# Layer 0's experts: VectorE's 32x32 block transposes in place of TensorE's products by the identity

## The reference

```python
def expert_choice_ffn(h, router_w, router_b, w_gate, w_up, w_down):
    cap = EC_CAPACITY * n // N_EXPERTS            # 64 latent rows, 32 context rows an expert
    affinity = jax.nn.softmax((h @ router_w + router_b).astype(F32), axis=-1)
    gates, idx = lax.top_k(jnp.swapaxes(affinity, 1, 2), cap)
    xg = jax.vmap(lambda hb, ib: hb[ib])(h, idx)
    hid = jax.nn.silu(jnp.einsum('becd,edf->becf', xg, w_gate)) * jnp.einsum('becd,edf->becf', xg, w_up)
    y = jnp.einsum('becf,efd->becd', hid, w_down) * gates[..., None].astype(h.dtype)
    scatter = lambda yb, ib: jnp.zeros((n, d), h.dtype).at[ib.reshape(-1)].add(yb.reshape(-1, d))
    return jax.vmap(scatter)(y, idx)
...
        f_l = expert_choice_ffn(modulate(rmsnorm(x, ...), mod_l[3], mod_l[4]), ...)
        if ctx_out:                               # layer 0 only
            f_c = expert_choice_ffn(modulate(rmsnorm(ctx, ...), mod_c[3], mod_c[4]), ...)
```

## Time and profile before

| | us |
|---|---|
| median of three runs | 2111.51 |
| lowest, highest | 2110.48, 2114.74 |
| the profiled execution, span | 2111.8 |
| layer 0's experts, from the first latent product to the last down product | 608.96 to 1133.86 |
| one expert in the middle of layer 0 | 33.28 |

### The profile page before, as it was taken

The page is one execution under the profiler, slowest core; times in us unless marked ns, Lnnn a source line. Parts: engine busy times, 40 slices in busy tenths (PEclk is TensorE's granted clock), DMA queues, the critical chain, the costliest instruction groups (busy, mean ns, idle before and its releaser), DMA issues. The chain is left out here.

```text
span 2111.8 us, 25962 instructions
## 1 busy us (share of the span) xinstructions
PE 1960.2 (93%) x10890; PEld 956.5 (45%) x10890; DVE 679.0 (32%) x1283; ACT 518.4 (25%) x1016; POOL 187.9 (9%) x216
## 2 busy tenths in 40 slices
PE   5998999999989999999999999999898998888886
PEld 2656565544433333333335865655445333333322
DVE  2258552372431110111113476522524111111112
ACT  4146541452210000000004265514321100000012
POOL 1300000110011211212002000001100000000000
PEclk9999999999999999999999999999999999999999
DMA  9420303322199999999999223023419999999995
GB/s 350 143 80 1 140 1 130 110 90 110 65 344 402 394 399 396 393 402 393 402 395 302 84 80 140 1 92 148 163 61 358 399 408 409 409 408 409 409 409 221
DMA packets 164756, 530.63 MB, mean 251 GB/s; under 512 B 10968, under 2 KB 19490, under 8 KB 164642
## 3 DMA queue, kind: packets, MB, share of 16 engines
q1 hardware_dynamic: 149296, 489.49, 59.6%
q0 software_dynamic: 15120, 39.43, 6.0%
q10 hardware_dynamic: 226, 0.07, 0.0%
HBM read 507.98 MB, written 20.97 MB: 250 GB/s over the span
## 5 line engine op out<-in xcount | busy, mean ns | idle before, releaser
L3108 PE MATMUL ps<-ring,arena 128*64 128x512 f32 x1040 | 237.0, 608 | 22.1 <-DMA ring<-in_w_up 21.6
L2353 PE MATMUL ps<-arena,ring 128*128 128x256 f32 (+1 forms) x640 | 194.8, 465 | 2.4 <-DMA ring<-in_w_in 2.4
L3108 PE MATMUL ps<-arena 128*64 128x512 f32 x720 | 166.3, 609 | 11.9 <-DMA resid<-in_w_up 7.1
L2353 PEld LDWEIGHTS ps<-arena,ring 128*128 128x128 f32 x640 | 122.0, 192 | 76.9 <-issue 64.2
L3108 PEld LDWEIGHTS ps<-ring,arena 128*64 128x64 f32 x1040 | 77.6, 139 | 168.8 <-issue 167.5
L2935 PE MATMUL ps<-ring,arena 128*128 128x512 f32 x320 | 141.9, 597 | 0.6 <-ACT arena L1410 0.6
L2245 DVE TENSOR_TENSOR arena<-arena,ps 128x512 f32<-128x512 f32 x32 | 22.0, 688 | 311.7 <-ACT arena L1455 311.7
L1455 ACT ACTIVATE arena<-ps 128x512 f32<-128x512 f32 x32 | 19.1, 598 | 393.1 <-PE ps L3108 393.1
L3147 PE MATMUL ps<-ring,arena 128*64 128x512 f32 x496 | 111.9, 596 | 0.7 <-ACT arena L1485 0.7
L3108 PEld LDWEIGHTS ps<-arena 128*64 128x64 f32 x720 | 53.2, 140 | 113.9 <-issue 113.9
L1047 ACT ACTIVATE arena<-ps 128x768 f32<-128x768 f32 (+6 forms) x111 | 80.0, 725 | 88.0 <-PE ps L2371 45.2
(11 more groups left out here) (398 smaller groups left out, 2668.8 us busy)
## 6 DMA issues: line engine op xcount, KB each, us to landing
ring<-in_w_up SPq DMA_DIRECT2D x33, 2048.0 KB, 16.0
ring<-in_w_gate SPq DMA_DIRECT2D x32, 2048.0 KB, 20.8
ring<-in_w_down SPq DMA_DIRECT2D x31, 2048.0 KB, 23.0
ring<-in_ada_w SPq DMA_DIRECT2D x24, 2048.0 KB, 11.7
arena<-in_w_down SPq DMA_DIRECT2D x19, 2048.0 KB, 20.3
arena<-in_w_gate SPq DMA_DIRECT2D x18, 2048.0 KB, 20.4
arena<-in_w_up SPq DMA_DIRECT2D x12, 2048.0 KB, 13.6
ring<-in_w_in SPq DMA_DIRECT2D x6, 2048.0 KB, 13.5
```

What stands on the lines that cost most here:

```text
L2353: ins = mm(o[0:n, c0:c1], w[:, k, col:col + n], hT[:, k, c0:c1], start=k == 0, stop=k == KD - 1)
L3108: ins = mm(px[0][hf * 64:hf * 64 + 64, col:col + 512], xl[e % 2][:, at:at + CAP_L], w[c][:, hf * 512:hf * 512 + 512], start=b + c == 0, st ...
```

## The change

In layer 0 (`ctx_on`) the rows are laid out so that turning 32 x 32 blocks in place is enough, and VectorE's block transpose does it from SBUF to SBUF:

- the normed rows are stored with their columns in the order (a, k, r), where the feature is k * 128 + a * 32 + r (`token_row`);
- the latents are gathered in quarters: two DMAs an expert of 128 x 256 each, from row numbers `row_quarter`, which eight small products and two VectorE instructions make from the final `rows`;
- gate and up are computed with a stationary operand of 128 x 32 and a moving operand of 256 columns, the ones of `a`: eight runs of 32 with gaps (`by_quarters`), four products side by side;
- `context_rows_turned`, `context_hidden_turned` and, in layer 0, `latent_rows_turned` and `hidden_turned` are gone from TensorE, and with them ScalarE's and VectorE's copies; VectorE has `turned_rows`, `hidden_ctx_out` and `hidden_lat_out` with `dve.transpose`.

```diff
+            def gather_quarters(e):
+                for h in range(2):
+                    at = bass.IndirectOffsetOnAxis(ap=row_quarter[:, h * NE + e:h * NE + e + 1], axis=0)
+                    pool.indirect_dma_start(got_l[e % 2][:, h * 256:(h + 1) * 256], None, quarters_in, at).then_inc(got_lat[e % 2], 16)
...
+                def turned_rows(dst, src, h, s, turned, done):
+                    dve.transpose(turned_blocks(dst, h), block_rows_of(src, h)).then_inc(S[turned], 1)
+                    x3, n = in_chunks(dst, 32 * h), 32 * h
+                    dve.wait_ge(*v.next(S[turned]))
+                    TT(x3, x3, cF[:, :, s].unsqueeze(2).to_broadcast([P, KD, n]), ALU.mult).then_inc(dve_step, 1)
...
-                dve.copy_predicated(rows[:, NE:2 * NE], nearer_.bitcast(U32), rows[:, 0:NE]).then_inc(dve_step, 1)
-                dve.wait_ge(*v.next(dve_step))
...
+                dve.copy_predicated(rows[:, NE:2 * NE], nearer_.bitcast(U32), rows[:, 0:NE]).then_inc(S["rows_final"], 1)
+                dve.wait_ge(S["rows_final"], l + 1)
+                if ctx_on:
+                    dve.tensor_copy(row_no[:, 0:NE], rows[:, NE:2 * NE])
+                    dve.wait_ge(S["rows_spread"], 1)
+                    dve.scalar_tensor_tensor(slots[:, 240:272], lg[:, 0:2 * NE], 2.0,
...
+                    dve.tensor_copy(row_quarter, slots[:, 240:272])
...
                 def hidden_ctx_out(e):
-                    dve.wait_ge(S["hid_ctx_turned"], n0 + e + 1)
-                    dve.tensor_copy(hT_c[e % 2], px[3][:, 768:1024]).then_inc(S["hidT_ctx"], 1)
+                    dve.wait_ge(S["hid_ctx"], n0 + e + 1)
+                    if e >= 2:
+                        dve.wait_ge(S["down_ctx"], n0 + e - 1)
+                    dve.transpose(in_chunks(hT_c[e % 2], 32), in_chunks(hid_c, 32)).then_inc(S["hidT_ctx"], 1)
+
+                def hidden_lat_out(e):
+                    dve.wait_ge(S["hid_lat"], n0 + e + 1)
+                    if e:
+                        dve.wait_ge(S["down_lat"], n0 + e)
+                    dve.transpose(turned_blocks(hT_l[0], 2), block_rows_of(hid_l, 2)).then_inc(S["hidT_lat"], 1)
...
                     for c in cs:
-                        at = (c % 2) * P + (2 * b + c // 2) * CAP_C
-                        for i, (w, hf) in enumerate(((gate, 0), (gate, 1), (up, 0), (up, 1))):
-                            ins = mm(px[1][32 * i:32 * i + 32, 0:512], xc[e % 2][:, at:at + CAP_C],
-                                     w[c][:, hf * 512:hf * 512 + 512], start=b + c == 0, stop=b * c == 3)
+                        at = (4 * b + c) * CAP_C
+                        for w, col in ((gate, 0), (up, 256)):
+                            for a in range(4):
+                                ins = mm(px[1][32 * a:32 * a + 32, col:col + 256], xc[e % 2][:, at:at + CAP_C],
+                                         by_quarters(w[c])[:, :, a, :], start=b + c + col == 0, stop=b * c == 3 and col > 0)
...
                     def lat(b, w, col):
 
+                        if ctx_on:
+                            for c in range(4):
+                                at = (4 * b + c) * CAP_L
+                                for h, a in itertools.product(range(2), range(4)):
+                                    ins = mm(px[0][32 * a:32 * a + 32, col + 256 * h:col + 256 * h + 256],
+                                             xl[e % 2][:, at + 32 * h:at + 32 * h + 32], by_quarters(w[c])[:, :, a, :],
+                                             start=b + c + h == 0, stop=b * c * h == 3)
+                            return ins
...
+                    pe.wait_ge(S["rows_final"], l + 1)
+                    for h, a in itertools.product(range(2), range(4)):
+                        ins = mm(lg[32 * a:32 * a + 32, h * NE:(h + 1) * NE], K[:, K_ID + 32 * h:K_ID + 32 * h + 32],
+                                 rows[:, NE:2 * NE], start=True, stop=True)
+                    ins.then_inc(S["rows_spread"], 1)
```

More of the change, by code:

```diff
@@ L632, in build, with by_quarters, token_row @@
         b1 = b0 + NE * 96
+        def by_quarters(ap):
+            return ap.rearrange("p (k a r) -> p k a r", k=KD, r=32)
+        def token_row(l, i):
+            row = htok[:, i, :]
+            return row.rearrange("p (a k r) -> p k a r", k=KD, r=32) if l < DEPTH - 1 else row
         fT = [ar(13312 + i * D, D) for i in range(2)]
@@ L687, in build @@
         got_c, xc, hT_c, y_c = ([ar(m1 + 512 * n + i * 256, 256) for i in range(2)] for n in (0, 1, 4, 5))
-        sg_c, hid_c = (ar(m1 + 1024 + i * 512, 512) for i in range(2))
+        sg_c, hid_c = (ar(m1 + 1024 + i * 512, 256) for i in range(2))
         last_homes = {"dead": ((0, 1, wqu[:, 0:1024]), (1, 2, wkv[:, 0:1024]), (2, 3, kc(K_COS, 1024)), (3, 4, mrows[:, :])),
@@ L986, in _ @@
                 pool.wait_ge(s_hst, 16 * (NT - CT) * (l + 1))
-                gather_lat(0)
-                gather_lat(1)
+                gather = gather_quarters if l < DEPTH - 1 else gather_lat
+                gather(0)
+                gather(1)
                 for e in range(2, NE + 3):
@@ L991, in _ @@
                         pool.wait_ge(S["lat_turned"], l * NE + e - 1)
-                        gather_lat(e)
+                        gather(e)
                         if l < DEPTH - 1:
@@ L2172, in _ @@
                 dve.wait_ge(*v.next(dve_step))
-                dve.copy_predicated(rows[:, NE:2 * NE], nearer_.bitcast(U32), rows[:, 0:NE]).then_inc(dve_step, 1)
-                dve.wait_ge(*v.next(dve_step))
-                if not ctx_on:
+                dve.copy_predicated(rows[:, NE:2 * NE], nearer_.bitcast(U32), rows[:, 0:NE]).then_inc(S["rows_final"], 1)
[4 more added lines that the diff above has]
+                    dve.scalar_tensor_tensor(slots[:, 240:272], lg[:, 0:2 * NE], 2.0,
+                                             K[:, K_ROW + 2:K_ROW + 3].to_broadcast([P, 2 * NE]), ALU.mult, ALU.add)\
+                        .then_inc(dve_step, 1)
+                    dve.wait_ge(*v.next(dve_step))
+                    dve.tensor_copy(row_quarter, slots[:, 240:272])
+                else:
                     for i in range(2):
@@ L2178, in _ @@
                         dve.tensor_copy(last_rows[r, :], rows[r, NE:2 * NE].rearrange("p (a b) -> p a b", b=2)[:, :, i])
-                dve.tensor_copy(row_no[:, 0:NE], rows[:, NE:2 * NE])
+                    dve.tensor_copy(row_no[:, 0:NE], rows[:, NE:2 * NE])
                 phase()
@@ L3116, in gate_up @@
                     ins = lat(0, up, 512)
-                    if e == 0:
+                    if e == 0 and not ctx_on:
                         latent_rows_turned(1)
@@ L3131, in gate_up, with hidden_turned @@
                     lat(1, up, 512).then_inc(S["gu_lat"], 1)
[L3133 to L3136 removed]
+                def hidden_turned(e):
                     pe.wait_ge(S["hid_lat"], n0 + e + 1)
@@ L3231, in _ @@
                     ins.then_inc(S["down_ctx"], 1)
-                latent_rows_turned(0)
+                if not ctx_on:
+                    latent_rows_turned(0)
                 def last_gate_rows():
@@ L3264, in _ @@
                         down(e - 1, BLOCKS[l].index((2, e - 1, 0)))
-                    hidden_turned(e)
+                    if not ctx_on:
+                        hidden_turned(e)
                     if e == (0 if ctx_on else NE - 2):
                         down(e, BLOCKS[l].index((2, e, 0)))
-                    if e + 2 < NE:
-                        rows_turned(e + 2)
+                    if not ctx_on and e + 2 < NE:
+                        latent_rows_turned(e + 2)
                 if ctx_on:
```

88 lines of the change are left out of this document (40 added, 48 removed).

## The result

| | before | after |
|---|---|---|
| median, us (4 runs each, side by side) | 2112.81 | 2122.11 |
| lowest, highest | 2110.48, 2114.74 | 2120.97, 2126.20 |
| profiled execution, span | 2111.8 | 2119.9 |

The ratio is 1.0047, with a 95% interval of 1.0035 to 1.0059: the changed kernel is slower by 9.3 us (7.4 to 12.5). The forecast was 2113, no change. The interval excludes the outcome that the prediction held likeliest, a change within 0.2%. 2122 lies inside the range, in the third rival's stretch of 2117 to 2122, but in part by luck: 4.0 us of the loss come from a stretch that is in no rival.

What follows compares the result with a forecast made beforehand. Weight loads bound layer 0's experts. Head +1.75 and fetches +1.9 against the 1.6 us lead start the last products 2.1 us later; 0.5 less in the tail nets +1.6: 2113.4 profiled, median 2113, range 2104 to 2124.

Steps and rivals of the forecast that it cites:

- the third rival: Head and loads: fetches hit the engine behind, or split gather lands late; +3 and +4 to +8, 2117 to 2122; 17%.
- What bounds the kernel: Layer 0's experts: the DMA queue is slower, landings 33.8 us an expert apart, issues paced by TensorE 33.3.
- TensorE's first wait for weights: Layer 0's experts: TensorE, needing 32.25 us an expert, waits for weights from roughly the eighth expert on.
- TensorE's products: Gate and up in layer 0's experts: new products at 56 ns a record, 0.6 us an expert added.
- The first product: Head: expert 0 starts 1.75 us later, at 610.7; bounds 0 to +3.
- The context's transpose: Head, before the search for the largest affinities: VectorE turns the context's first rows itself, +0.4 us.
- the spread row numbers: Head, after the final row numbers: eight small products, a multiply-add and a cast, +1.1 us.
- Expert 0's start taken as the restart of the loads: Head: expert 0's first product sets the start of the closed chain of transfers, so its 1.75 us carry over.
- The fetches: Load stage: 1.8 more an expert, 29 in all, 31 engine-us, +1.9 us if spread over 16 engines; ends 0 and +31.
- The tail: Behind the last landing: only the turning of expert 15's hidden rows goes, 0.5 us saved.
- the lead: End of layer 0's loads: 1.6 us left between the last landing and the products that wait for it.

Runs made afterwards that it cites:

- x5: Changed kernel with the latents' 32 wide products and one gather an expert, no spread row numbers, VectorE turnings kept: 2113.7 us, 1.0002 to the kernel before.
- x7: Kernel before with 12 more filler calls ahead of expert 0's first gate product, a delay of 4.9 us: 2115.2 us, 1.0012 to the kernel before.
- x2: Kernel before with only the change's number of calls (latents' products 32 by 256, context's halved), turnings and gathers as before: 2116.5 us, 1.0019 to the kernel before.
- x4: Changed kernel with gate and up products reading 256 weights in one run instead of eight gapped runs of 32: 2121.8 us, 1.0039 to the kernel before.
- x12: Changed kernel with GpSimd's six gathers for experts 2 and 3 held until expert 0's gate and up products end: 2122.2 us, 1.0045 to the kernel before.
- x1: Changed kernel with the latents' gate and up products wide again, 32 calls an expert for 128: 2116.6 us, 1.0021 to the kernel before.
- x3: Changed kernel with one gather instruction an expert, 2 KB pieces, and no spread row numbers: 2118.1 us, 1.0021 to the kernel before.
- x8: Wide latents' products kernel plus 48 tiny products an expert in experts 1 to 15, all in one column group: 2141.5 us, 1.0139 to the kernel before.
- x9: Kernel before with gate and up products cut in two along the weights' columns, 64 more calls an expert: 2111.4 us, 0.9994 to the kernel before.
- x10: Wide latents' products kernel plus 40 tiny products an expert in experts 1 to 15, over four column groups: 2117.8 us, 1.0026 to the kernel before.
- x6: Changed kernel with 32 tiny products ahead of expert 0's context down product and three fillers less: 2123.5 us, 1.0043 to the kernel before.
- x11: Changed kernel with three filler calls before the row numbers' turning replaced by 24 tiny products over four column groups: 2123.2 us, 1.0053 to the kernel before.

## Why the prediction was right and wrong

- **What bounds the kernel: right.** The loads were the slower resource. x5 saves TensorE's time and gains nothing; x7 passes a delay on to the end of the experts in full. TensorE's first wait for weights came in the sixth expert, where the eighth was forecast.
- **TensorE's products: right.** 55 to 56 ns a record. The 0.6 us an expert were not even added: x2, with all the split products, repeats an expert in 33.25 us for 33.28. By the Trainium skill's 60 cycles a product (TensorEngine Tiling (Array Packing), Performance Considerations) it would have been an estimated 5.7 us; the trace disagrees. The Trainium skill's rule on 16-byte lines (Advanced Engine Details and Errata, Memory Cachelines) agrees with x4, where eight runs of 32 read as fast as one of 256.
- **The first product: right,** +1.94 for +1.75. The context's transpose was +0.48 (0.4 forecast), the spread row numbers +0.65 (1.1), the rest the gather.
- **Expert 0's start taken as the restart of the loads: wrong, 4.0 us.** The prediction carried only the start of the first gate half forward ("Its start is set by expert 0's first product") and took its length as unchanged. It took 7.67 us for 3.69. The six gathers from 607.4 to 614.0 us beside it, twice as many for the latents as before and no longer held back by TensorE's turnings, were in the code to see; x12 shows that without them the stretch goes, x1 that it takes the many calls too.
- **The fetches: the number right, the size wrong, +1.9 for +5.6 us.** "31 engine-us, or +1.9 us if spread over the 16 engines": 29 fetches of 1.04 us each came, 30 engine-us. They were not spread. Measured from the restart, the eight pieces of the last load that land first came 0.9 us later than before (498.1 for 497.2), the eight that land last 5.3 us (507.4 for 502.1). 30.2 / 8 = 3.8 us is most of that, so the fetches fall on one half of the engines, and a block counts as landed only with its last piece. What is left of the 5.6, about 1.8 us, stays open: the two-part gather is 0.2 to 0.4 of it (x3; x1 against x5), and in every run but x8 the gap is somewhat larger than the fetches' time divided by eight (28 fetches, 29.0 / 8 = 3.6 for 4.9). The dose fits: 0.22 us a fetch in x9, 0.18 in x2, 0.19 in x10 over x1, 0.20 in the changed kernel. The trace doesn't name the engine of a packet, so that the fetches run on that half is inferred from the size, and which half it is and why stays open.
- **The argument against the third rival was the mistake.** "Nothing shows them bound to one engine": the trace of before showed the two groups already. The sixteen completions of one load, issued at 1099.4 before and at 1094.6 after, in us before the last of them:

```
before  6.5 6.4 6.0 5.9 5.8 5.4 5.4 5.2 | 1.7 1.5 1.5 1.4 1.3 0.1 0.0 0.0
after  11.2 11.1 11.0 11.0 10.9 10.7 10.6 10.3 | 2.3 2.2 1.9 1.9 1.7 1.4 0.4 0.0
```

  I had read the growing lag of the earlier trace rows as the rate of the whole queue. Part of it was one half of the engines falling behind: in the kernel before the gap is 1.4 us for the load issued at 683.1 and 4.9 for the one issued at 1082.5.
- **The tail: right,** -0.39 for -0.5, and the lead: 1.44 us for 1.6.

The Trainium skill says that crossing a boundary of 16 KB of instructions is mostly hidden (Runtime: NRT & Kernel Launch, Instruction fetch mechanics). Here it isn't: where the DMA engines set the pace, each costs some 0.2 us of the load stage.

## What to carry to other kernels

Where transfers set the pace, TensorE's time is free but its instructions are not: count the calls, turn them into fetches, and charge each to the half of the engines that is behind. A busy share of 100% on TensorE doesn't make it the bound: compare how far apart its experts start with how far apart the loads land. Look at the completions of the single pieces of a late load, not only at its last one; a gap there says which resource the next fetch will hit. And when a step on the path moves, look at what runs beside its whole length, not only at its start.

## What was not expected of the hardware

- **Instruction fetches slow eight of sixteen DMA engines.** Gap 4.9 us at 28 fetches, 6.2 at 34, 7.7 and 7.8 at 43 and 44, 9.1 to 10.5 at 57 to 59: some 0.17 us for each. Where TensorE was the bound (x8) it stayed at 1.0.
- **Back-to-back gathers by GpSimd can starve TensorE of instructions.** Four records each 0.72 us for 4.4 us, with the clock at 1.00 and the DMA engines 60% idle (window 611.7 to 616.1: share 0.40). It took six gathers in 6.6 us and 128 records beside them; with either made fewer there was no such stretch.
- **A short wait of TensorE sometimes costs its clock.** In layer 1 it waits 2.13 us ahead of a product in every run. In the kernel before the clock fell behind that wait, in x7 it did not, and from 1450 to 1482 us x7 gained 4.8 us on it (the same products of L2799 and L2813 start at 1449.58 and 1482.46 before, at 1451.68 and 1479.73 in x7). The windows of before and x7:

```profile
1460.00:1470.00 10.00, 7.87 (x32) 4.58 (x30) 2.18 (x4) 5.45 (x6) 1.04 (x1) 0.68 0.00 1
```
```profile
1460.00:1470.00 10.00, 7.61 (x43) 3.98 (x42) 2.60 (x3) 7.12 (x8) 2.19 (x3) 1.00 0.00 0
```

  Behind the experts, the four profiled executions that kept the clock there (x6 to x9) took 972.9 to 973.9 us, the ten others 977.7 to 979.5. Of the other executions only the clock is on record: of the 21 of the kernel before that ran beside x5 to x8, the fastest (2109.8 us) and the slowest (2115.8) have a mean granted clock of 0.984 and 0.978. So the clock is likely most of the spread of the times here, and the reason why 2 us of a change can be seen in the experts' stretch and not in the whole time.
- **Tiny products like neighbours.** 128x16 products took 35 to 36 ns a record in one column group (x8), 18 to 20 ns when spread over four (x10, and the spread row numbers of the changed kernel), 12.5 in one row of 48 (x11).
